# Expert weights loaded as pairs of neighbouring units, 2 MB in one transfer, in the order in which their places come free

## The reference, cut to what matters

```
for e in range(N_EXPERTS):            # 8
    y = y + combine[..., e:e+1] * swiglu(h, w_gate[e], w_up[e], w_down[e])
swiglu(h, wg, wu, wd) = (silu(h @ wg) * (h @ wu)) @ wd
w_gate, w_up: (8, 1024, 3584)    w_down: (8, 3584, 1024)    float32
```

## Time and profile before

| What | Value |
|---|---|
| median of three runs | 1401.55 us (1401.47 to 1401.76) |
| the profiled execution | 1401.67 us |
| its span, first to last instruction | 1399.8 us |
| TensorE busy | 1350.1 us (96%) |
| mean granted TensorE clock | 0.998 of full speed |
| bytes moved | 456.33 MB, mean 326 GB/s |
| transfer engines in the last 25 of 40 slices | nine tenths or more in 24 of them |

### The profile page before, as it was taken

One profiled execution on the slowest core, in us unless ns is written; L12 is line 12 of the kernel. 1 busy time (PEld: TensorE's weight loads), 2 busy tenths in 40 slices (PEclk: granted clock), 3 DMA queues, 4 the chain that ended last, 5 costly groups with the idle time before them and its releaser, 6 DMA issues.

```text
span 1399.8 us, 21441 instructions
## 1 busy us (share of the span) xinstructions
PE 1350.1 (96%) x9122; PEld 699.4 (50%) x9122; DVE 486.7 (35%) x722; ACT 493.6 (35%) x842; POOL 22.2 (2%) x61
## 2 busy tenths in 40 slices
PE   9999999999999999999989999999889999999886
PEld 8887888888898785333322333333222233333221
DVE  5777855555666863111111111111111111111123
ACT  6566454344556644213222223113112113213112
POOL 1000000000000003000000000000000000000100
PEclk9999999999999999999999999999999999999999
DMA  9933655537554339999999999999999999999995
GB/s 350 347 113 121 204 179 189 180 120 242 169 199 136 143 122 421 410 421 420 409 420 408 420 420 421 409 421 421 409 421 421 406 421 421 409 420 420 419 422 216
DMA packets 95542, 456.33 MB, mean 326 GB/s; under 512 B 7656, under 2 KB 13304, under 8 KB 52432
## 3 DMA queue, kind: packets, MB, share of 16 engines
q1 hardware_dynamic: 91280, 443.13, 79.9%
q10 hardware_dynamic: 2704, 6.97, 1.5%
q0 software_dynamic: 1456, 4.79, 0.9%
HBM read 446.47 MB, written 8.39 MB: 325 GB/s over the span
## 4 chain that ended last, share of the span: by engine, by line
PE 73%; DMA 19%; DVE 3%; ACT 2%; issue 1%; SPq 1%; ACTq 0%; DVEq 0%
PE A L508 23%; PE DN L508 12%; PE A L497 7%; DMA raw_more<-in_moe_w_up 7%; PE A L499 7%; PE A L498 7%; DMA raw_more<-in_moe_w_gate 4%; DMA raw_more<-in_moe_w_down 4%; PE A L503 3%; DMA raw<-in_moe_w_down 2%; DMA raw<-in_moe_w_up 2%; PE DN L499 1%; PE DN L497 1%; PE DN L498 1%; PE DN L503 1%; PE T L2201 1%
## 5 line engine op out<-in xcount | busy, mean ns | idle before, releaser
L508 PE MATMUL A<-raw_more,heTf 128*32 128x512 f32 x2160 | 257.9, 594 | 4.2 <-DMA raw_more<-in_moe_w_up 1.9
L472 DVE TENSOR_TENSOR wlo<-raw,whi 128x2048 fp32r<-128x2048 f32 (+3 forms) x83 | 180.0, 2175 | 94.2 <-ACT whi L465 94.2
L465 ACT ACTIVATE whi<-raw 128x2048 fp32r<-128x2048 f32 (+3 forms) x83 | 150.8, 1821 | 99.3 <-PE A L499 56.5
L497 PE MATMUL A<-whi,hTh 128*128 128x512 f32 (+2 forms) x448 | 174.4, 389 | 1.5 <-DVE wlo L1137 0.9
L498 PE MATMUL A<-wlo,hTh 128*128 128x512 f32 (+2 forms) x448 | 170.0, 380 | 0.0
L499 PE MATMUL A<-whi,hTl 128*128 128x512 f32 (+2 forms) x448 | 170.0, 379 | 0.0
L1013 ACT ACTIVATE aTf<-T 128x384 f32<-128x384 f32 (+1 forms) x56 | 25.2, 450 | 381.1 <-PE T L2201 381.1
L508 PEld LDWEIGHTS A<-raw_more,heTf 128*32 128x32 f32 x2160 | 71.7, 110 | 160.7 <-issue 149.4
L508 PE MATMUL A<-raw,heTf 128*32 128x512 f32 x1200 | 150.3, 593 | 0.4 <-DMA raw_more<-in_moe_w_up 0.4
L1595 DVE TENSOR_TENSOR sg<-A,pT 96x512 f32<-96x512 f32 x35 | 24.0, 687 | 363.0 <-ACT pT L985 363.0
L508 PE MATMUL DN<-raw_more,aTf 128*32 128x512 f32 x1056 | 118.2, 593 | 0.4
(11 more groups left out here) (355 smaller groups left out, 1645.9 us busy)
## 6 DMA issues: line engine op xcount, KB each, us to landing
raw_more<-in_moe_w_gate SPq DMA_DIRECT2D x73, 1024.0 KB, 27.4
raw_more<-in_moe_w_up SPq DMA_DIRECT2D x72, 1024.0 KB, 27.3
raw_more<-in_moe_w_down SPq DMA_DIRECT2D x71, 1024.0 KB, 27.6
raw<-in_moe_w_down SPq DMA_DIRECT2D x41, 1024.0 KB, 27.4
raw<-in_moe_w_up SPq DMA_DIRECT2D x40, 1024.0 KB, 27.4
raw<-in_moe_w_gate SPq DMA_DIRECT2D x39, 1024.0 KB, 27.1
raw<-in_w_in SPq DMA_DIRECT2D x22, 1024.0 KB, 6.7
raw<-in_dense_w_down SPq DMA_DIRECT2D x11, 1024.0 KB, 5.0
```

Source lines behind the costliest of these rows:

```text
L465: nc.scalar.activation(split_slot(u)[0][:, :n], raw_of(u, e)[:, :n], ACT.Copy).then_inc(hi_done, 1)
L472: nc.vector.tensor_tensor(lo[:, :n], raw_of(u, e)[:, :n], hi[:, :n].bitcast(F32), ALU.subtract).then_inc(lo_done, 1)
L497: nc.tensor.matmul(o, hi, wh, start=start, stop=False)
L508: return nc.tensor.matmul(o[at * QUARTER:(at + 1) * QUARTER], tokens, w, start=start, stop=stop, tile_position=(0, at * QUARTER))
```

## The change

The 17 places become 18, as nine pairs of neighbours of 16 KB per partition, and one transfer fills a pair with two units. Its source is one run of 2 MB, with 16 KB per partition. For that the host lays gate and up weights out together, one half of the rows of a group for gate beside the same half for up, and the two down units of a group together.

- The nine pairs are three over raw (six places), one called LOW over oTl and mg, one over qT and kT, one over hTh and hTl, and three over the split parts. For the last, whi and wlo now lie interleaved in one buffer (parts). aTf moves behind LOW.
- The first round takes the pairs in the order [QK_PAIR, 0, 1, LOW, 2], then the three over the split parts in the order in which TensorE frees them, then the one over hTh and hTl. The raw places are numbered from unit 85 back (raw_slot), so raw pair 0 holds units 79 and 80, pair 1 units 81 and 82, and pair 2 units 83 and 84.
- A pair is loaded again when TensorE has used both its units (used_by). The order of matmuls is as before. A small expert still takes gate, gate, up, up, which is now the first unit of one pair, the first of the next, the second of the first, the second of the next, so the first pair of a group comes free after three units.
- Both units of a pair count as landed when the whole transfer has.
- One pair instead of two places is kept back for the last expert.
- The units before the experts are loaded as they were.

```diff
-        BACK_SLOTS = (W_SLOT, W_SLOT + 1)
-        FIRST_SLOTS = [R + 1, R + 2, 0, 1, 2, 3, R, 4, 5] + [W_SLOT + s + k for s in range(S) for k in (0, S)] + [R + 3, R + 4]
+        BACK_PAIR = W_PAIR
+        FREED_W = [W_PAIR + u % S for u in range(UM - S, UM)]
+        FIRST_PAIRS = [QK_PAIR, 0, 1, LOW, 2] + FREED_W + [H_PAIR]
+        PAIRS = NE * EU // 2
+
+        def raw_slot(u):
+
+            return (u - UM) % R
...
+        def used_by(g):
+
+            e, i = 2 * g // EU, 2 * g % EU
+            first = [UM + e * EU + group_at(j) for j in range(EG)]
+            return UM + 2 * g + (3 if is_small(e) and UM + 2 * g in first else 2)
...
+            def load_pair(g, src):
+
+                pair, held, _ = PLACED[g]
+                if held is not None:
+                    sp.wait_ge(unit_used, used_by(held))
+                elif pair < LOW:
+                    sp.wait_ge(lo_done, UM - R + 2 * pair + 2)
+                elif pair == LOW:
+                    sp.wait_ge(unit_used, at[1, "out"])
+                    sp.wait_ge(mg_T[1], 4)
+                elif pair == QK_PAIR:
+                    sp.wait_ge(scored[1], MLA_FILLS)
+                elif pair == H_PAIR:
+                    sp.wait_ge(unit_used, UM)
+                else:
+                    sp.wait_ge(unit_used, max(u for u in range(UM) if u % S == pair - W_PAIR) + 1)
+                sp.dma_start(pairs[pair][:].rearrange("p w n -> p (w n)"), src).then_inc(pair_landed[pair], 16)
...
-                            small_products(e, u + h, h, A[j % 2], j == 0)
+                            small_products(e, u + 2 * h, h, A[j % 2], j == 0)
...
-                            small_products(e, u + 2 + h, h, A[2 + j % 2], False)
+                            small_products(e, u + 1 + 2 * h, h, A[2 + j % 2], False)
```

More of the change, by code:

```diff
@@ L197, in sem @@
             return ctx.enter_context(nc.semaphore(name))
+        o_raw = used[0]
         raw = place("raw", [P, R, UNIT], F32)
         o_w = used[0]
-        whi = place("whi", [P, S, UNIT], F32R)
-        wlo = place("wlo", [P, S, UNIT], F32R)
+        parts = place("parts", [P, S, 2, UNIT], F32R)
+        whi, wlo = parts[:, :, 0, :], parts[:, :, 1, :]
         xs = place("xs", [P, NB, D], F32)
@@ L251, in trunk @@
         kT = place("kT", [P, HEADS, SEQ], F32)
-        raw_more = [place(f"raw_more{i}", [P, UNIT], F32, o) for i, o in enumerate(
-            [o_pj, o_qT, o_kT, o_h, o_h + 4 * UNIT] + [o_w + 4 * UNIT * i for i in range(2 * S)])]
+        pairs = [place(f"pair{i}", [P, 2, UNIT], F32, o) for i, o in enumerate(
+            [o_raw + 8 * UNIT * i for i in range(R // 2)] + [o_o + 8192, o_qT, o_h] + [o_w + 8 * UNIT * i for i in range(S)])]
         o_bg = used[0]
@@ L409, in in_main @@
             return UM <= u < UM + NE * EU
-        BACK_SLOTS = (W_SLOT, W_SLOT + 1)
-        FIRST_SLOTS = [R + 1, R + 2, 0, 1, 2, 3, R, 4, 5] + [W_SLOT + s + k for s in range(S) for k in (0, S)] + [R + 3, R + 4]
+        BACK_PAIR = W_PAIR
[4 more added lines that the diff above has]
+            return (u - UM) % R
         def place_loads():
[L416 to L419, removed]
+            order = list(FIRST_PAIRS)
+            held = {}
+            loads = [sum(raw_slot(u) == s for u in range(UM)) for s in range(0, R, 2)] + [1] * (len(pairs) - R // 2)
@@ L420, in place_loads @@
             placed = {}
[L421 to L427, removed]
+            for g in range(PAIRS):
+                pair = next(i for i in order if g < PAIRS - EU // 2 or i != BACK_PAIR)
+                order.remove(pair)
+                order.append(pair)
+                loads[pair] += 1
+                placed[g] = (pair, held.get(pair), loads[pair])
+                held[pair] = g
@@ L450, in raw_there @@
                 return 16 * (u // R + 1)
-            if u < UM + NE * EU:
-                return 16 * PLACED[u + times(e, EU) - UM][2]
-            return 16 * (LOADS[u % R] + (u - UM - NE * EU) // R + 1) + times(e, 16 * EU // R)
+            if in_main(u):
+                return 16 * PLACED[pair_of(u)][2]
+            slot = raw_slot(u)
+            before = LOADS[slot // 2] if slot % 2 == 0 else sum(raw_slot(v) == slot for v in range(UM))
+            return 16 * (before + (u - UM - NE * EU) // R + 1) + times(e, 16 * EU // R)
         def split_slot(u):
@@ L625, in expert_loads @@
             def expert_loads(base, e, which):
-                gate, up, dn = (w[bass.ds(which, 1)].rearrange("a u p k n -> p (a u) k n")
-                                for w in (moe_w_gate, moe_w_up, moe_w_down))
+                columns, rows_down = pairs_of(which)
                 i = 0
```

134 lines of the change are left out of this document (60 added, 74 removed).

## The result

The changed kernel takes 1388.13 us (median of four, 1386.42 to 1390.77) against 1401.55: a ratio of 0.9906 (95% interval 0.9890 to 0.9922), 13.4 us faster. In a second measurement it was 1388.61, ratio 0.9908 (0.9893 to 0.9923). The forecast was 1381.0, 20.6 us faster. The direction and the bound are right; the gain is two thirds of it, outside the forecast's own range (1376 to 1387) and inside the wide one (1375 to 1394). The profiled execution shown here is the slowest of the four (1390.77, span 1389.0). One of the five executions of experiment 8's kernel took 2231.43 us, at a mean granted clock of 0.575, and is left out of its median.

A forecast was written before the change was run, and what follows sets the result against it. The prediction took the transfer engines to bound the kernel. Its terms, -10.1 - 12.2 + 1.7 = -20.6 us, gave 1381.0 against the median of 1401.55, with its own range 1376 to 1387 (0.62) and a wide one of 1375 to 1394.

The forecast's parts named there:

- What bounds the kernel: Transfer engines set the end: they never pause, while TensorE alone would be done at 1335, 50 us before the last landing.
- Part 1, the early start: First round of weight loads starts earlier: 58.0 units instead of 53.3 by 651.48, net of a gap -10.1 us.
- The issue times: First-round pairs issued at about 495, 507.5, 509.0 (LOW) and 513.8, then near 515, 521 and 526.7 us.
- The gap behind it: Transfers pause as the small second expert begins, since the next pair comes free only after three units: 1.7 us.
- Part 2, the pieces: 16 KB pieces instead of 8 KB save 0.044 us per unit over 278 units behind the first expert: -12.2 us.
- rival C: Larger packets are slower and the kernel loses, 1428 at 5% slower; tokens and outputs on other queues have slack; chance 0.07.
- Part 3, the tail: At the end of the last expert, two units instead of one stand behind the last landing: +1.7 us.
- A: Head start alone; 16 KB pieces are cut again or have no smaller fixed cost: -8.4 us, 1393; chance 0.17.
- B: Rate alone; coarser freeing of places eats the head start, 56 units at 651.5: 1386, or 1391 if fully gone; chance 0.11.
- D: Nothing changes: rate loss and head start cancel within 0.2% (2.8 us), only by chance; chance 0.03.
- The share: Transfer share falls to about 0.93 in the first expert, then is 1.0 from about 658 to the last landing.
- The clean rate: Weight stream in clean stretches runs at 427 to 429 GB/s where it was 421.

The follow-up runs named there:

- experiment 8: Changed kernel with each pair of the last expert loaded as two 1 MB transfers in 8 KB pieces, each with its own landing: 1387.2 us.
- experiment 4: Kernel before, with its 17 single places and 1 MB transfers, only the first round reordered as places come free: 1393.88 us.
- experiment 3: Changed kernel with the early start undone (raw pair 2 put second in the first round), pieces and pairs kept: 1395.4 us.
- experiment 1: Changed kernel with each pair still one 2 MB transfer, but its source laid out as two runs, giving 8 KB pieces: 1395.04 us.
- experiments 10 and 11: 56 extra 128 KB loads added to the kernel of experiment 6 (low partitions 1434.83 us, high 1433.81) and to that of experiment 1 (low, 1435.04).
- experiment 6: Changed kernel with small experts taking gate, up, gate, up in their matmuls, so a pair comes free after two units: 1386.22 us.

## Why the prediction was right, and where its sizes were off

**What bounds the kernel.** Right. TensorE's work is the same, and the time followed the transfers in every experiment.

**Part 1, the early start.** Forecast -10.1 us; measured -7.7 alone (experiment 4) and 7.3 lost when undone (experiment 3). The issue times were right. One size was off. At the end of the first expert 57.3 units were there, not 58.0: I let the full places hide the token traffic altogether, but the stream only just caught up with it, and 0.7 unit is 1.8 us. The gap behind it was about as forecast: by 727.2 the changed kernel is 3.4 units ahead of the one before (90.10 against 86.49 MB), 8.6 us. The single-place kernel had 59.53 / 1.0486 = 56.8 units at 651.5, 3.5 more than before, and was 3.1 ahead at 727.2 (89.71 MB), 7.7 us, which is what it gained in the end. The 18th place and the pairs have no part in that.

**Part 2, the pieces.** This is the mis-sized term: forecast -12.2 us, measured -6.9 (experiment 1). A part of the miss is the price of a packet. The line through the earlier trace rows gave 12.8 ns, from which I took 0.044 us per unit; the three sizes give 8.5 to 10 ns and 0.034 to 0.040 us, 9.5 to 11.1 us over 278 units. The early stretch of 9 to 20 us was a bad second point, for its packets were of mixed sizes; what else its mean time held was not looked into. The rest, 2.6 to 4.2 us, is that the saving doesn't hold where other queues are at work. The small transfers take turns with packets twice as long, and the stream then gains nothing (396 against 399 GB/s around a token load), with 0.15 us more lost per 128 KB load (experiments 10 and 11), and the six token loads behind the first expert cost it 1.6 to 3.9 us more than with 8 KB packets, about the size of this rest. I had named this under rival C as having slack, which is true of who waits for the tokens, and not of the stream. The estimate of 3.5 ns per packet that I worked out from the Trainium skill (DMA: Bandwidth & Descriptors, "Why small descriptors are slow") would have given 3.9 us; the measured 8.5 to 10 ns lie between it and my line.

**Part 3, the tail.** Forecast +1.7 us. The net price of pairs against singles in the same order is 1.2 us (experiments 1 and 4), so the term is right in size. But the tail of the changed kernel doesn't hang where I put it. I wrote that the last group needs no more time; in fact its second gate and up pair, with the three units that wait for it and the down units behind them, ended last in both profiles. In the first profile four pairs of matmuls there ran at the half clock, 1.7 us more. The matched order of matmuls is 1.9 us faster (experiment 6), about 1 us of it because the stream gets its places back sooner. The granted clock wasn't in my sum at all. It was 1.00 in all of the earlier trace rows, and I had named the longer starving of TensorE without asking what it does to the clock.

**The sum.** By the experiments it is -7.7 - 6.9 + 1.2 = -13.4, the measured gain. That they add up proves nothing: they are the steps of one path, from the kernel before to experiment 4's, to experiment 1's, to the changed one, and such steps always sum to the whole. What backs them is that the counts of units agree with the first two. Of the 7.2 us that the forecast was too large, 5.3 belong to the pieces, 2.4 to the early start, and the tail gives back 0.5.

**Rivals.** A (the early start alone) falls with experiment 1. B falls with experiment 3 and with the 57.3 units at 651.5, where it had 56. C falls, since the clean stream is 1.2% faster (27.59 against 27.26 MB), but its side remark on other queues holds in part. D, a change within 0.2%, was not the case.

**What would show it.** The share was to fall below 1 through the first expert; it did so only at its two ends. The clean rate was to be 427 to 429 GB/s and was 427. TensorE was to starve in the fifth and eighth experts, hardly in the second: it did, 75.09 us busy of 75.7 in the second where it had been 72.72.

```profile
651.50:727.20 75.70, 75.09 (x366) 25.52 (x364) 15.72 (x23) 19.61 (x40) 0.00 (x0) 1.00 0.99 408
```

A pair was to land 7 to 8 us after its issue in the first expert, and took 8.5 us or more. The last landing was to be at 1363.5 and came at 1371.

## What to carry to other kernels

When a stream of loads bounds the kernel, read the first round of its buffers first: one buffer that comes free last, put early in the ring, held up all loads behind it, and moving it gave more than half of the gain with one line. Price a change of packet size from two clean stretches of the same kind, and don't apply the saving to the time in which other queues share the engines. And when loads come in larger steps, let their consumer take them in the order in which they land. Otherwise it idles longer at a time, and it gives the first place of a group back later. Here the two together were worth 1.9 us.

## What the runs showed of the hardware that was not expected

- A packet has a fixed price on its transfer engine beside its bytes: 9.0 ns between 4 and 8 KB, and 8.5 to 10 ns between 8 and 16 KB.
- A load of 64 rows of 2 KB from another queue, beside a full weight stream, costs the stream 0.71 us with 8 KB packets in it and 0.87 us with 16 KB, 2.3 and 2.8 times what its bytes are worth. It doesn't matter which half of the partitions it fills.
- In the last 8 to 10 us of the stream the transfer engines run at about half rate in every kernel looked at. Which engines are late, and why, was not found. By my estimate, half of these 8 to 10 us, it costs 4 to 5 us at the end of each of these streams.
- TensorE fell to 1.2 GHz in parts of the small experts of the changed kernel, where it did one unit (1.7 us) and then stood for up to 4.7 us. Its busy time alone doesn't show the loss, for matmuls at the half clock count as busy for longer: in 1300:1340 it was busy 33.96 us with 142 matmuls at a granted clock of 0.87 there, and 32.83 us with 150 at 1.00 in the kernel before:

```profile
1300.00:1340.00 40.00, 32.83 (x150) 10.31 (x150) 7.34 (x10) 6.98 (x13) 3.85 (x4) 1.00 1.01 420
```
